# The last stage of a hybrid encoder layer, joined to the experts stage: gate, weighted sums and last store moved

## What is computed

```python
x = x + (1 + gate2) * hierarchical_moe(h)       # two experts of 32 per token, each token with two weights
out = rms_norm(x, final_norm_g) * (1 + scale_f) + shift_f
```

## Time and profile before

| what | us |
|---|---|
| median of 3 runs | 1998.74 |
| lowest and highest | 1995.21, 2001.17 |
| the profiled execution | 1998.57 |
| its span (first to last recorded instruction) | 1996.7 |
| mean granted TensorE clock, share of full speed | 0.913 |

### The profile page before, as it was taken

How to read it: one execution, slowest core, us unless ns; L and a number is a source line. 1 busy time by engine, 2 the same in 40 slices (tenths; PEclk the granted TensorE clock), 3 DMA queues, 4 the chain that set the end, 5 groups by cost and what they waited for, 6 DMA issues and landing times. The chain is left out here.

```text
span 1996.7 us, 40655 instructions
## 1 busy us (share of the span) xinstructions
PE 1606.4 (80%) x16134; PEld 1064.4 (53%) x16135; DVE 869.5 (44%) x1904; ACT 605.6 (30%) x1169; POOL 397.8 (20%) x825
## 2 busy tenths in 40 slices
PE   3899999967778788878886996487889996999920
PEld 2744444336656567666663454354556664666610
DVE  2257686346666766766642122221212221222228
ACT  3213886712423334434430222011111111111112
POOL 7331457601110110110100000111111111111123
PEclk8899999978889999999997996698989998999965
DMA  9493534320021010010003645399999999999755
GB/s 308 165 381 128 189 119 156 114 79 26 13 67 58 13 36 26 13 36 7 7 7 102 246 169 200 110 358 372 375 364 343 329 341 343 357 338 335 240 197 187
DMA packets 195983, 362.07 MB, mean 181 GB/s; under 512 B 29984, under 2 KB 67920, under 8 KB 195856
## 3 DMA queue, kind: packets, MB, share of 16 engines
q1 hardware_dynamic: 158128, 305.98, 44.4%
q0 software_dynamic: 37728, 54.34, 8.8%
HBM read 303.48 MB, written 56.64 MB: 180 GB/s over the span
## 5 line engine op out<-in xcount | busy, mean ns | idle before, releaser
L1837 PE MATMUL psX<-arena 128*64 128x256 f32 x1536 | 192.3, 408 | 49.8 <-DMA arena<-in_e_down_dram 48.2
L1837 PEld LDWEIGHTS psX<-arena 128*64 128x64 f32 x1536 | 121.6, 148 | 134.0 <-issue 89.8
L1861 PE MATMUL psP<-arena 128*64 128x512 f32 x768 | 175.4, 599 | 0.0
L1799 DVE SCALAR_TENSOR_TENSOR arena<-arena,psX 128x256 f32<-128x256 f32 x48 | 20.2, 422 | 347.3 <-ACT arena L1770 341.5
L792 PE MATMUL psP<-arena 128*128 128x512 f32 x320 | 142.8, 601 | 2.9 <-DVE arena L693 2.9
L792 PE MATMUL psX<-arena 128*128 128x512 f32 x320 | 142.6, 601 | 1.9 <-DVE arena L693 1.9
L487 ACT ACTIVATE arena<-arena 128x1024 bf16<-128x1024 f32 (+5 forms) x138 | 134.2, 973 | 32.5 <-POOL arena L444 28.6
L1774 ACT ACTIVATE arena<-psP 128x512 f32<-128x512 f32 x48 | 28.7, 597 | 378.9 <-PE psP L1861 378.9
L1748 POOL DMA_DIRECT2D expert_rows<-arena x48 | 41.7, 869 | 497.0 <-ACT arena L1774 468.1
L889 POOL TENSOR_TENSOR st<-st,mhalf 128x8 f32<-128x8 f32 x16 | 27.2, 1698 | 535.1 <-DVE st L1105 418.4
L1642 PE MATMUL psP<-arena 128*128 128x512 f32 x256 | 115.9, 612 | 15.8 <-DMA arena<-mix_T 10.7
(11 more groups left out here) (399 smaller groups left out, 2770.8 us busy)
## 6 DMA issues: line engine op xcount, KB each, us to landing
arena<-in_e_gate_dram SPq DMA_DIRECT2D x32, 2048.0 KB, 10.0
arena<-in_e_up_dram SPq DMA_DIRECT2D x32, 2048.0 KB, 24.7
arena<-in_e_down_dram SPq DMA_DIRECT2D x32, 2048.0 KB, 23.6
arena<-in_ada_w_dram SPq DMA_DIRECT2D x12, 2048.0 KB, 15.1
expert_rows<-Z POOLq DMA_DIRECT2D x34, 512.0 KB, 17.5
expert_rows<-arena POOLq DMA_DIRECT2D x48, 256.0 KB
proj_T<-arena SPq DMA_DIRECT2D x36, 256.0 KB, 2.0
arena<-in_x_dram SPq DMA_DIRECT2D x16, 512.0 KB, 7.1
```

What stands on the lines that cost most here:

```text
L1799: dve.scalar_tensor_tensor(out=hid, in0=hid, scalar=1.0, in1=psum["X0"][:, 0:DE // 2], op0=ALU.add, op1=ALU.mult).then_inc(q("half_gated"), 1)
L1837: mm = pe.matmul(psum["X0"][BLK * h:BLK * h + BLK, 0:DE // 2], xT[:, k, :], gate_w[u][:, k, DE // 2 * h:DE // 2 * (h + 1)], start=(k == 0) ...
L1861: mm = pe.matmul(psum["P0"][BLK * half:BLK * half + BLK, :], hidT[:, f, h, :], down_w[u][:, KE // 2 * h + f, D // 2 * half:D // 2 * (half ...
```

## The change

The finish phase goes, and its work is put behind the experts in the same block, with waits on semaphores in place of the barrier.

- The gate row is multiplied into each block's rows where they leave PSUM: `evict` on VectorE takes the place of ScalarE's move, and stands between the gated steps of one block and those of the next. The gate row (in halves) and the two rows of the final norm are loaded by SyncE at the start of the experts stage, into SBUF tiles that are free by then.
- The last block's store is issued by SyncE, the others by GpSimd as before. For that the number of whole pairs less one (`full`) is computed in the router.
- `first`, `second` and `x1` lie in the weight slots 1 and 2, the smaller buffers in slot 0.
- SyncE: last store, `x1` loads (from the third on each behind the first gather of two tiles before), then the out stores. GpSimd: all 16 gathers in a row, with the power of tile t-4 behind the gathers of tile t. ScalarE: 16 diagonal matrices, each the identity times a weight of the tile's tokens, then the squares. TensorE: four matmuls a tile with these diagonals sum the two expert rows in PSUM. VectorE: adds `x1` from PSUM, then variance and writing as before.

```diff
                 step(dve.tensor_scalar(pairs, blocks, 1, None, ALU.logical_shift_right))
+                step(dve.tensor_scalar(first_block[:, NE + 2:NE + 3], pairs, 1, None, ALU.subtract))
...
# SyncE, start and end of the experts block
+                for h in range(2):
+                    sp.dma_start(gate_half[BLK * h:BLK * h + BLK, :], mod_d[1:2, 512 * h:512 * h + 512].to_broadcast([BLK, 512])).then_inc(q("gate_half"), 16)
+                for i, dst in ((2, shift_row), (3, gain_row)):
+                    sp.dma_start(dst, mod_d[i:i + 1, :].to_broadcast([P, D])).then_inc(*sig("rows_loaded", i, by=16))
...
+                sp.wait_ge(q("y_ready"), pairs * 2 + 1)
+                sp.dma_start(y_d[bass.ds((full * 2 + 1) * BLK, BLK), :].rearrange("r (h n) -> h r n", h=2), y_sb[1]).then_inc(q("last_stored"), 16)
+                for t in range(NT):
+                    if t >= 2:
+                        sp.wait_ge(*at(f"gathered0{t - 2}", 0))
+                    sp.dma_start(x1[:, t, :], x1_d[tile(t), :]).then_inc(*sig(f"x1_loaded{t}", 0, by=16))
+                for t in range(NT):
+                    sp.wait_ge(*at("out", t))
+                    sp.dma_start(out[0, tile(t), :], normed[:, t % 2, :]).then_inc(*sig(f"out_stored{t % 2}", t, by=16))
...
# GpSimd
+                pool.wait_ge(q("y_stored0"), pairs * 16)
+                pool.wait_ge(q("y_stored1"), full * 16)
+                pool.wait_ge(q("last_stored"), 16)
+                pool.sem_inc(q("stores_seen"))
+                for t in range(NT):
+                    for j, dst in enumerate((first, second)):
+                        pool.indirect_dma_start(dst[:, t, :], None, y_d[:, :], bass.IndirectOffsetOnAxis(ap=dest[:, t, j:j + 1], axis=0))\
+                            .then_inc(*sig(f"gathered{j}{t}", 0, by=16))
+                    if t >= 4:
+                        roots(t - 4)
+                for t in range(NT - 4, NT):
+                    roots(t)
...
# ScalarE
-                        act.activation(y_sb[j], psum["P0"], ACT.Copy).then_inc(q("y_ready"), 1)
+                act.wait_ge(q("y_ready"), pairs * 2 + 1)
+                for t in range(NT):
+                    for j in range(2):
+                        link(act, act.activation(weigh[:, t, j, :], ident[:, :], ACT.Copy, scale=wgt[:, t, j:j + 1]), "weights", t, j)
+                for t in range(NT):
+                    act.wait_ge(*at("x2", t))
+                    link(act, act.activation(junk, res[:, t % 2, :], ACT.Square, accum_out=s_x[:, t:t + 1]), "x_squares", t)
...
# VectorE
+                def evict(b, j, stored):
+                    dve.wait_ge(q("y_done"), b + 2)
+                    if stored is not None:
+                        dve.wait_ge(q(f"y_stored{j}"), stored)
+                    dve.tensor_tensor(y_sb[j], psum["P0"], gate_half, ALU.mult).then_inc(q("y_ready"), 1)
...
+                with dve.Fori(1, full) as i:
+                    evict(i * 2 + 1, 1, i * 16)
+                    gated(i * 2 + 2)
+                    evict(i * 2 + 2, 0, i * 16 + 16)
+                    gated(i * 2 + 3)
+                evict(full * 2 + 1, 1, full * 16)
...
+                def add(t):
+                    dve.wait_ge(*at("combined", t))
+                    dve.wait_ge(*at(f"x1_loaded{t}", 0))
+                    if t >= 2:
+                        dve.wait_ge(*at("x_squares", t - 2))
+                    link(dve, dve.tensor_tensor(res[:, t % 2, :], psum["PTXW"[t % 4]], x1[:, t, :], ALU.add), "x2", t)
...
+                add(0)
+                variance(0)
+                for t in range(NT):
+                    if t + 1 < NT:
+                        add(t + 1)
+                    write(t)
+                    if t + 1 < NT:
+                        variance(t + 1)
...
# TensorE
+                for t in range(NT):
+                    if t >= 4:
+                        pe.wait_ge(*at("x2", t - 4))
+                    for j, rows_of in enumerate((first, second)):
+                        pe.wait_ge(*at("weights", t, j))
+                        pe.wait_ge(*at(f"gathered{j}{t}", 0))
+                        for half in range(2):
+                            part = slice(512 * half, 512 * half + 512)
+                            mm = pe.matmul(psum["PTXW"[t % 4] + str(half)], weigh[:, t, j, :], rows_of[:, t, part], start=(j == 0), stop=(j == 1))
+                    mm.then_inc(*sig("combined", t))
```

More of the change, by code:

```diff
@@ L1689, in sparse_attention_moe_layer @@
             gate_w, up_w, down_w = zip((A.take(KD, DE), A.take(KD, DE), A.take(KE, D)), *others)
+            A.at = 0
+            first, second, x1 = (A.take(NT, D) for _ in range(3))
+            assert A.at == (SLOTS - 1) * (2 * KD * DE + KE * D)
+            A.at = WEIGHTS_AT
+            res, normed, junk, weigh = A.take(2, D), A.take(2, D), A.take(D), A.take(NT, 2, P)
+            gate_half, shift_row, gain_row = ckvT[:, 0:512], kiT[:, :], ckv_all[:, :, :].rearrange("p t c -> p (t c)")
+            s_x = st[:, 0:32]
+            tile = lambda t: slice(P * t, P * t + P)
             q = S.sem
@@ L1809, in _, with variance, write @@
                     scale_rows(b + 1)
-                for j in range(2):
-                    dve.wait_ge(q(f"y_stored{j}"), pairs * 16)
-                    dve.tensor_copy(hid[:, j:j + 1], y_sb[j][:, 0:1])
+                scale_rows(0)
+                dve.wait_ge(q("gate_half"), 32)
+                gated(0)
+                evict(0, 0, None)
+                gated(1)
+                evict(1, 1, None)
+                gated(2)
+                evict(2, 0, 16)
+                gated(3)
+                with dve.Fori(1, full) as i:
[10 more added lines that the diff above has]
+                    link(dve, dve.tensor_tensor(res[:, t % 2, :], psum["PTXW"[t % 4]], x1[:, t, :], ALU.add), "x2", t)
+                def variance(t):
+                    dve.wait_ge(*at("x_squares", t))
+                    link(dve, dve.tensor_scalar(s_x[:, 8 + t:9 + t], s_x[:, t:t + 1], 1.0 / D, NORM_EPS, ALU.mult, ALU.add), "x_var", t)
+                def write(t):
+                    b = t % 2
+                    dve.wait_ge(*at("x_rstd", t))
+                    if t >= 2:
+                        dve.wait_ge(*at(f"out_stored{b}", t - 2))
+                    if t == 0:
+                        dve.wait_ge(*at("rows_loaded", 3))
+                    step(dve.scalar_tensor_tensor(out=normed[:, b, :], in0=res[:, b, :], scalar=s_x[:, 16 + t:17 + t], in1=gain_row, op0=ALU.mult, op1=ALU.mult))
+                    link(dve, dve.tensor_tensor(normed[:, b, :], normed[:, b, :], shift_row, ALU.add), "out", t)
+                add(0)
[6 more added lines that the diff above has]
+                        variance(t + 1)
             @block.tensor
```

135 lines of the change are left out of this document (29 added, 106 removed).

## The result

The changed kernel takes 1989.91 us (median of 7 runs, 1985.96 to 1995.12) against 2001.17 for the kernel before (7 runs): ratio 0.9947, 95% interval 0.9927 to 0.9967. It is faster, by 11.3 us; 22 had been predicted, to 1977 (range 1966 to 1987). The profiled execution took 1988.95, its span is 1987.1 us, 9.6 less than that of before.

What follows compares the result with a forecast made beforehand. Experts stage bound by TensorE, DMA close behind; the stage after it by VectorE behind DMA. Span 1973.7 + 0.2 + 1.0 = 1974.9, 21.8 under 1996.7; 1998.57 - 21.8 gives 1977 us, range 1966 to 1987.

Steps and rivals of the forecast that it cites:

- part 5: Gathers and tile 0: GpSimd's queue of ten gathers delays tile 0's power by 2 us; writing starts at 1931.1.
- part 3: Eviction with the gate on VectorE in the experts stage: hidden by 3.9 us of slack, priced at 0; uncovered 33 us.
- part 6: SyncE's order, x1 loads ahead of the first out store: VectorE stands still 7.5 us before tile 2's writing.
- part 2: Start of the experts stage: four broadcast loads share DMA with the first row fetch, +1.0 us (0 to 3.3).
- a sign of being wrong: Check on the experts stage: the prediction is wrong if its 632 us move by more than 3.
- Part 4: Last store by SyncE: issued 1911.15, two engines, landed 1917.75, first gather 1917.9 (ends 1913.3 and 1920.6).
- Rival A: Quicker, 1965 to 1972 us: last store lands like other SyncE stores, or the stall before tile 2 doesn't come, or both; 17%.
- Part 7: Period of the later tiles: 4.2 us a tile against 7.19, with the power beside the add costing nothing.
- check from above: Whole gain seen roughly: 5.0 us from earlier gathers, about 21 from the shorter period, less the stall before tile 2.
- Rival B: Gathers in the last stage keep their old pace of 3.2 us each: measured 1986 us; 15%.
- C: Slower than before: VectorE's eviction waits for a late store in the experts stage; full cost gives 2010 us; 3%.
- D: All open terms at upper ends: store +2.7, gathers +4, power +1.8, start +2.3: 1988 us; 2% for this or beyond.

Runs made afterwards that it cites:

- k1: The kernel before plus only the four broadcast start loads (1.3 MB) at the start of the experts stage, into unread tiles: 2004.8 us, ratio 1.0024.
- k10: The changed kernel with VectorE's eviction made twice in each block, the first into a tile nobody reads: 1990.4 us, ratio 0.9949.
- k3: The changed kernel with the last store issued as two transfers of 64 rows by 512 columns: 1982.7 us, ratio 0.9921.
- k5: The changed kernel with all eight x1 loads moved ahead of the last store, behind expert 29's down product: 1981.0 us, ratio 0.9903.
- k4: The changed kernel with x1 tiles 0 to 4 loaded first, then each out store followed by one more x1 load: 1983.1 us, ratio 0.9911.
- k11: The kernel of k12 plus 40 small unused matmuls on TensorE ahead of the first gathered rows: 1966.6 us, ratio 0.9837.
- k12: The changed kernel with late start loads, early x1 loads and the last store in two transfers: 1969.5 us, ratio 0.9855.

## Why the prediction was wrong

The direction was right and the gain about half. What failed are the sizes of parts 2, 4 and 6, the reading of a row in part 5, and perhaps the zero of part 3. The largest miss in the rewritten stage is the landing of the last x1 load and the first out store (part 6); of the misses ahead of it that have a shown cause, the largest is the start loads (part 2). By the prediction's own parts, on the profiled execution:

- *Part 2, the start loads: mis-sized.* 1.0 was taken from bounds of 0 and 3.3; the fetch lost 3.2, the upper bound, and k1 shows that it stays to the end. The sharing at half rate that was assumed didn't happen: the fetch was in use only 1.2 us after the last of the 1.3 MB had landed (1280.0, by its 5.7 us from issue to landing on the page). The profile also issued the fetch 1.5 us later than before's (0.2 predicted), and the steps behind it took 0.4 less, so the first product is 4.3 later and not 1.2.
- *Part 3, the eviction: priced at 0.* The cover that it named is there (48 of 48 waits for TensorE; k10, doubled, makes no difference; 11.69 us between products). The stage is nevertheless 3.3 us longer in this pair of profiles, which is over the 3 us that the prediction gave as a sign of being wrong. Stages of the same code differ by up to 3.3 us and those of kernels alike in it by 6; what part of the 3.3 is the change stays open.
- *Part 4, the last store: choice right, size short.* 6.75 us from issue to first gather were predicted and 8.73 measured; the eviction and SyncE's issue came on time. k3 shows the two-engine shape as the cause, k5 that the loads behind it add nothing. The row of 9.2 us for this very tile was the nearer price: the 0.8 ahead of the transfer and 0.5 behind it came from no row. Rival A's quick store was wrong.
- *Part 5, tile 0: the count of matmuls was wrong.* The row of 24 matmuls in 10.46 us counts records, and a 128x512 float32 matmul has two. The four matmuls of a tile cost 3.6 us at full clock, twice what was predicted, and an estimated 7 at half, where records come 0.85 us apart. Writing of tile 0 starts 15.3 us after the first gather (13.2 predicted). The working also left out that the add of tile 1 stands ahead of it. The wait for GpSimd's queue named there didn't decide: at 1940.79 GpSimd had been idle for 1.22 us.
- *Part 6, SyncE's order: right in place and cause, short in size.* 10.28 us idle before tile 2's writing, 7.5 predicted; k4 and k5 confirm the cause. From the first gather to the last x1 load it took 24.5 us (23.6 predicted). The x1 load and the out store then took 9.1 us (1951.90 to 1961.03) and not 5.4. They were given 60% of the DMA rate, from a stretch of before in which up to eight x1 loads were queued at once; at the 414 GB/s measured here from 1955 to 1960, 9.1 us are an estimated 3.8 MB, and their 1.05 MB are 28% of it.
- *Part 7, the period: right.* 4.03 against 4.2. The power took 0.55, as "Who interferes with whom" in "SBUF — State Buffer" of the Trainium skill has it for a VectorE instruction with at most one input in SBUF: it doesn't contend with GpSimd.

The misses in order of time: start +3.1, stage +3.3, seam +1.9, tile 0 +2.1, from there to tile 2's writing +2.5, the last tiles -0.7: 12.2 us, from 1974.9 to the span of 1987.1. Tile 2's writing hangs on the gather of tile 5 and the out store. Counted along that chain, the 4.6 us of tile 0 and the stall are 0.9 up to the last x1 load and 3.7 behind it. Whether tile 0's lateness cost anything at the end isn't shown, since the gather that it held back by 1.22 us went into a DMA at a share of 1.0. The prediction's check from above (5.0 and 21, less the stall of 7.5) gives 18.5 and doesn't confirm its 21.8.

Rival B (the gathers at their old pace) came near in time by luck: the DMA share was 1.0 as it says, but the gathers didn't keep their pace (the last was in use at 1963.22, 35.8 us after the first one's issue, where B has 53.6), and the last writing waited for none. C didn't occur. Of D's open terms two did come near their upper ends, the start (+2.2 of 2.3) and the store (+2.0 of 2.7); the other two, tile 0's gathers and the power, added nothing.

## What to carry to other kernels

- Loads put at the start of a stage, where DMA is idle, stand in front of that stage's first fetch: 1.3 MB cost 3 us of a 2000 us kernel. Issue them behind the first fetches.
- Moving a slow transfer to another queue doesn't mend its shape. Look at the DMA share while it runs: 0.13 is 2 engines of 16. Two transfers of 64 rows took 3.8 us where one of two halves took 8.7.
- When stages are merged into one in-order stream, list what stands ahead of the first store. Here eight loads did, and with two buffers for the written tile that became 10 us of idle VectorE.
- Before a row of matmuls is used as a price, count how many records one instruction of that type leaves.

## What the runs showed of the hardware

- A 128x128 by 512-column float32 matmul shows as two records (eight for the four matmuls of a tile; 80 for k11's 40 small ones).
- TensorE's granted clock was 1.00 (2.4 GHz) at the last product, fell to 0.50 (1.2 GHz) while TensorE stood still, and was 0.82 on the mean from 1935 to 1940, with tile 0's sums running since 1931.77. With k11's 40 small matmuls in between it stayed at 1.00. The same eight records took 6.17 us in the changed kernel, 5.24 in k12 and 3.60 in k11.
- VectorE's add with one operand in PSUM went with a power on GpSimd of 0.55 us, the add with both in SBUF with one of 1.60.
- The experts stage, with the DMA share at 0.98, differs by 0.8 to 3.3 us between two profiles of one kernel (619.1 and 619.9; 614.5 and 616.4; 614.9 and 618.2; 617.2 and 619.1), and by 6 among kernels whose stage has the same instructions (616.1 to 621.9). A single pair of profiles can't price an edit of a few us there.
- A 256 KB store whose outermost dimension is 2 took 8.7 us from issue to use with nothing beside it (k5) and 9.2 on GpSimd's queue; as two transfers of 64 rows it took 3.8 (k3).
